# A weight ring with a fourth output tile outside it, paired modulation chunks, later raw loads and fewer waits, in a streaming trunk on one NeuronCore

## The chip, the core and the metric

The kernel runs on one NeuronCore of a Trainium2 chip. The metric is the device time of one launch in microseconds (us), and lower is better. TensorE (PE) multiplies matrices; VectorE (DVE), ScalarE (ACT) and GpSimd (POOL) do the elementwise work; SyncE (SP) issues every DMA from one queue, in the order in which the program lists them, and waits on semaphores between them.

## What is computed

One inference step of two layers over 2048 prompt tokens and 32 sample tokens, with a model width of 1024, all in float32. Layer 0 is a pooling mixer, layer 1 is sliding-window attention. Scale, shift and gate of each layer come from a modulation, a vector-matrix product with a 1024 x 3072 matrix for each layer.

```python
def trunk(x, c, sample):
    for i in range(DEPTH):                                    # DEPTH = 2
        shift, scale, gate = modulation(c, ada_w[i], ada_b[i])   # silu(c) @ ada_w + ada_b, in three
        h = rms_norm(x, norm_g[i]) * (1 + scale[:, None]) + shift[:, None]
        if i % 2 == 0:      # u, gate = h @ w_in; pooled windows of u; z = pooled @ w_grp
            y, st = pool_mixer(...)   # y = (z * scale * silu(gate)) @ w_out
        else:               # q, k, v, gate = h @ w_in; banded attention with sinks and ALiBi
            y, kw, vw = attn_...(...) # y = (o * silu(gate)) @ w_out
        x = x + gate[:, None] * y
    return rms_norm(x, final_g), pool states, k windows, v windows
```

## The kernel before

**Tiles and units.** The 2048 tokens are worked in four parts of 512; part 0 also carries the 32 sample tokens and is cut into two blocks of 272 columns. First the pooling layer runs over parts 0 to 3, then attention runs over parts 0 to 3: eight stages. A weight tile is 128 output channels by 1024 inputs. A unit is one weight tile against one block of tokens: eight k-steps, and in each of them three matmuls (`split_product`, L921), because float32 is made of a high and a low half of weights and of activations: hi x hi, hi x lo, lo x hi. A full unit is thus 24 matmuls of 512 columns.

**A pooling stage** goes through four groups g. Each group has two u units (u0, u1), two gate units (gate0, gate1), and two short z units (six matmuls each) that share one small `grp` tile; after the four groups come eight output units. **An attention stage** has four groups of kv, q0, q1, g0, g1 units, with the scores (S), transposes and products of the attention items between them, and then eight output units (`aout` 0 to 7). The first four of them (three in the `ps_u` banks, one in `ps_s`) run k-steps 0 to 5 while the last items are still being finished, then k-steps 6 and 7, and only then follows the fifth.

**The weight ring.** Four slots (`RING`) of `w_hi` and `w_lo` hold split tiles. Tile j goes to slot j % 4, and it is asked for (step `WL`) right behind the last unit that uses tile j - 4: SP waits until that unit is done (`tile_used`, L735 to L748 and L774) and then issues two DMAs of 512 KB (`fetch_tile`, L779 and L780). In the first use of a tile it is loaded raw, split by ACT and POOL and stored to DRAM (`keep_tile`); from then on both halves are fetched from there.

**The early split.** The first 24 tiles of attention (`fore`: kv, q, gate tiles and `aout` 0 to 3) are split during pooling stages 1 to 3, eight in each: step FL loads a raw tile into one of two buffers (`fore_raw`, L742, L744 and L748), FW splits it (ACT, then POOL in place), FS stores both halves (L840, L841). FL of tile i + 2 waits until FS of tile i has landed, since it overwrites its buffer. In a group, FW comes behind u0 and gate0, FS behind u1 and gate1, each FS followed at once by the FL of the tile two further on.

**The modulation** is read in 48 chunks of 512 KB (L792). 16 come ahead of the first stage; the other 32, eight in each pooling stage, go through three buffers: one ADA step is eight small matmuls with a chunk (L952), and on SP the ADA step of chunk i issues the load of chunk i + 2. Steps ADA stand behind u0, u1 and gate0 of groups 0 and 1, and behind u1 and gate0 of group 2.

**What sets the order.** Nothing is scheduled at run time: class `Schedule` writes one list of steps, and each engine walks that list and does its share. SP too takes its steps in list order, so a wait on SP holds all DMAs behind it. On PE every unit waits for its bank, its weights (`w_fetched`, or `w_hi_ready` and `w_lo_ready`) and, at each k-step, for both halves of the activations, for instance:

```python
n = KT * u["s"] + k + 1
pe.wait_ge(h_hi_ready, n)
pe.wait_ge(h_lo_ready, n)
```

Of the kernel before, what the change touches and what calls it, by code (L numbers as in the profile page):

```python
# [18 lines left out]
F32 = mybir.dt.float32  # L19
# [6 lines left out]
P = 128  # L26
# [53 lines left out]
class Schedule:  # L80
# [10 lines left out]
    def __init__(self):  # L91
# [25 lines left out]
        load_after = {self.last_unit[j - RING]: j for j in range(RING, len(self.tiles))}  # L117
        steps, self.steps = self.steps, []
        for st in steps:
            self.steps.append(st)  # L120
            if st[0] == "U" and st[3] == KT and st[1] in load_after:
                self.steps.append(("WL", load_after[st[1]]))
# [77 lines left out]
    def pool(self, p):  # L200
# [46 lines left out]
        for g in range(GROUPS):  # L247
            for i in range(2):
                emit(self.group(p, self.tile(("pin", 2 * g + i)), "u", n=2 * g + i, g=g, i=i))
                if i == 0:  # L250
                    self.early(p, 2 * g)
                else:
                    self.early_out(p, 2 * g)
                if g < 2:
                    self.ada(1)
                elif g == 2 and i:
                    self.ada(1)
                if i == 1:
                    s.append(("PL", p, g, 0))
            late, lower = [], []  # L260
            for i in range(2):
# [176 lines left out]
def trunk_kernel(nc, I, O):  # L438
# [3 lines left out]
    with ExitStack() as ctx:  # L442
# [92 lines left out]
        w_fetched = [sem(f"w_fetched{i}") for i in range(RING)]  # L535
# [31 lines left out]
        kept, home, fore = sched.kept, sched.home, sched.fore  # L567
# [12 lines left out]
        def keeps(j):  # L580

            return sum(1 for i in kept if i <= j and i % RING == j % RING and own(i))
# [7 lines left out]
        def fetches(j):  # L590

            return sum(1 for i in range(j + 1) if i % RING == j % RING and not own(i))
# [11 lines left out]

        def bank_of(u):
# [6 lines left out]
        loads, per_slot = [], [0] * RING  # L612
        for j, t in enumerate(tiles):
            if own(j):
                per_slot[j % RING] += 32 if t[0] == "kv" else 16
            loads.append(per_slot[j % RING])
# [113 lines left out]
        def _(sp):  # L730
# [20 lines left out]
            def load_tile(j):  # L751

                t = tiles[j]
                if j >= RING:
                    tile_used(sp, j - RING)
                    if own(j - RING):
                        sp.wait_ge(w_kept[j % RING], 32 * keeps(j - RING))
                load_raw(t, w_raw[:, j % RING, :], raw_loaded[j % RING])

            def keep_tile(j):  # L760
# [4 lines left out]
                sp.dma_start(w_hi_dram[i, :, 0:n], w_hi[:, j % RING, 0:n].bitcast(F32)).then_inc(w_kept[j % RING], 16)  # L765
                sp.dma_start(w_lo_dram[i, :, 0:n], w_lo[:, j % RING, 0:n].bitcast(F32)).then_inc(w_kept[j % RING], 16)

            def fetch_tile(j):

                i, n = kept.index(home[j]), width[j]  # L770
                tile_used(sp, j - RING)
# [3 lines left out]
                else:  # L775
                    sp.wait_ge(w_kept[home[j] % RING], 32 * keeps(home[j]))
                if own(j - RING):
                    sp.wait_ge(w_kept[j % RING], 32 * keeps(j - RING))
                sp.dma_start(w_hi[:, j % RING, 0:n].bitcast(F32), w_hi_dram[i, :, 0:n]).then_inc(w_fetched[j % RING], 16)  # L779
                sp.dma_start(w_lo[:, j % RING, 0:n].bitcast(F32), w_lo_dram[i, :, 0:n]).then_inc(w_fetched[j % RING], 16)  # L780
# [124 lines left out]
        def _(pe):  # L905
# [26 lines left out]
            for st in steps:  # L932
# [68 lines left out]
                elif kind == "U":  # L1001
# [22 lines left out]
                    if own(j):  # L1024
                        pe.wait_ge(w_hi_ready, splits(j))
                        pe.wait_ge(w_lo_ready, splits(j))
                    else:
                        pe.wait_ge(w_fetched[j % RING], 32 * fetches(j))
                    bank = ps_u[u["bank"]] if u["bank"] < 3 else ps_s[:, u["bank"] - 3, :]
                    slot = j % RING  # L1030
                    if u["kind"] == "z":
# [4 lines left out]
                            (w_hi[:, slot, a:a + P], w_lo[:, slot, a:a + P], q_st[:, k, c0:c0 + w], q_st[:, 2 + k, c0:c0 + w])  # L1036
                            for k, a in enumerate(at)])
                    else:
# [7 lines left out]
                        for k in range(k_from, k_to):  # L1046

                            if u["kind"] != "out":
# [7 lines left out]
                            else:  # L1056
# [4 lines left out]
                                (w_hi[:, slot, k * P:(k + 1) * P], w_lo[:, slot, k * P:(k + 1) * P],  # L1061
# [450 lines left out]
        def _(act):  # L1512
# [6 lines left out]
            for st in steps:  # L1519
                kind = st[0]  # L1520
                if kind == "W":

                    j = st[1]
                    act.wait_ge(raw_loaded[j % RING], loads[j])
                    A(w_hi[:, j % RING, 0:width[j]], w_raw[:, j % RING, 0:width[j]], ACT.Copy).then_inc(w_hi_ready, 1)  # L1525
# [242 lines left out]
        def _(pool):  # L1768
# [8 lines left out]
            for st in steps:  # L1777
                kind = st[0]
                if kind == "W":
# [4 lines left out]
                    pool.wait_ge(raw_loaded[j % RING], loads[j])  # L1784
                    G.tensor_tensor(w_lo[:, j % RING, 0:width[j]], w_raw[:, j % RING, 0:width[j]],  # L1785
                                    w_hi[:, j % RING, 0:width[j]].bitcast(F32), ALU.subtract).then_inc(w_lo_ready, 1)
# [107 lines left out]
```

## Time and profile before

| | |
|---|---|
| time, median of 3 runs | 1662.85 us (1662.7 to 1666.46) |
| the profiled execution's own time | 1663.97 us |
| its span, first to last instruction | 1662.2 us, mean granted clock 0.983 |
| PE busy | 1572.7 us (95%) |
| DVE, ACT, POOL busy | 826.7, 729.9, 421.6 us (50%, 44%, 25%) |
| DMA moved | 342.10 MB, 58.4% of 16 engines' span on SP's queue |
| mean DMA rate, pooling stages 1, 2, 3 | 293, 287, 277 GB/s (share 0.83, 0.81, 0.79) |
| mean DMA rate, attention stages 1, 2, 3 | 152, 154, 135 GB/s (share 0.43, 0.43, 0.39) |

The first stage begins at 50 us, pooling stages 1 to 3 lie between 220 and 748 us, attention after that; its stage 1 ends near 1205, stage 2 near 1415. A busy PE is not a PE at its peak: matmuls overlap in the records, and what counts is how far their starts are apart. The profile counts an engine's idle time from the modelled end of its last matmul, some 0.17 us later than the next one could have started. A wait that the profile puts down to "issue" on PE is one that it can't name a releaser for; a DMA's landing is often behind it.

### The profile page before, as it was taken

The numbers are of one execution on the slowest core, as the hardware profiler recorded it, in microseconds if no ns is written. First come the engines' busy times: TensorE is split into PE (matmuls) and PEld (weight loads), VectorE is DVE, ScalarE is ACT, GpSimd is POOL, SyncE is SP. The second block draws the span as 40 slices with busy tenths as digits, with TensorE's granted clock in tenths as the row PEclk, the third lists the DMA queues.
The fourth block names the chain that finished last, engine by engine and source line by source line (L and its number), as shares of the span: only waits on it lengthen the run. The fifth ranks groups of instructions, "written<-read, shape, count | busy, mean of one in ns | idle before, by whom it ended". The sixth has DMA issues, their size and how long they took to land.

```text
span 1662.2 us, 28381 instructions
## 1 busy us (share of the span) xinstructions
PE 1572.7 (95%) x9355; PEld 1319.7 (79%) x9355; DVE 826.7 (50%) x2154; ACT 729.9 (44%) x1618; POOL 421.6 (25%) x403
## 2 busy tenths in 40 slices
PE   5899999989999999999889899999899998999997
PEld 2899987777777877888888798888788887888876
DVE  2556335323434344336666634666346664366651
ACT  3444433223232333235555454656436664456642
POOL 0342421112111211112222241333213333123332
PEclk9899999999999999999999999999999999999998
DMA  8787788886888778962222275334463334643313
GB/s 286 267 291 262 265 302 289 299 318 229 281 325 286 272 278 289 335 242 103 103 104 102 102 256 188 142 129 153 151 203 128 128 137 167 211 149 129 131 67 135
DMA packets 174519, 342.10 MB, mean 206 GB/s; under 512 B 22127, under 2 KB 89023, under 8 KB 174126
## 3 DMA queue, kind: packets, MB, share of 16 engines
q1 hardware_dynamic: 174382, 340.29, 58.4%
q8 instruction: 84, 1.38, 0.3%
q14 instruction: 53, 0.43, 0.1%
HBM read 266.13 MB, written 74.31 MB: 205 GB/s over the span
## 4 chain that ended last, share of the span: by engine, by line
PE 75%; DMA 7%; DVE 6%; ACT 4%; issue 3%; SPq 2%; POOL 1%; POOLq 0%; DVEq 0%; ACTq 0%
PE ps_u L921 59%; DMA w_lo_kept<-fore_raw 4%; PE ps_o L1153 4%; PE ps_s L1107 3%; PE ps_t L1126 3%; ACT work L1726 1%; DMA work<-in_x_prompt_dram 1%; DVE work L1453 1%; PE ps_s L921 1%; ACT ps_u L1625 1%; PE ps_s L952 1%; DMA chunks<-in_ada_w_dram 1%; DMA w_raw<-in_pool_w_out_dram 1%; PE ps_t L1166 1%; DVE ps_u L1308 1%
## 5 line engine op out<-in xcount | busy, mean ns | idle before, releaser
L921 PE MATMUL ps_u<-h_all_hi,w_hi 128*128 128x512 f32 (+2 forms) x1440 | 520.4, 361 | 11.9 <-DVE h_all_lo L1238 4.4
L921 PE MATMUL ps_u<-h_all_lo,w_hi 128*128 128x512 f32 (+2 forms) x1440 | 511.2, 355 | 0.0
L921 PE MATMUL ps_u<-h_all_hi,w_lo 128*128 128x512 f32 (+2 forms) x1440 | 510.8, 355 | 0.0
L921 PEld LDWEIGHTS ps_u<-h_all_hi,w_hi 128*128 128x128 f32 x1440 | 274.2, 190 | 66.5 <-issue 22.7
L921 PEld LDWEIGHTS ps_u<-h_all_hi,w_lo 128*128 128x128 f32 x1440 | 274.1, 190 | 36.9
L921 PEld LDWEIGHTS ps_u<-h_all_lo,w_hi 128*128 128x128 f32 x1440 | 274.1, 190 | 34.5
L1308 DVE TENSOR_TENSOR ps_u<-ps_u,rstd_b 128x512 f32<-128x512 f32 (+1 forms) x180 | 107.1, 596 | 274.4 <-PE ps_u L921 266.9
L921 PE MATMUL ps_u<-y_hi,w_hi 128*128 128x512 f32 (+1 forms) x600 | 218.4, 364 | 16.0 <-issue 10.6
L1866 POOL TENSOR_TENSOR work<-work,recip 128x512 f32<-128x512 f32 (+2 forms) x136 | 132.9, 997 | 360.3 <-DVE recip L1470 360.3
L921 PE MATMUL ps_u<-y_hi,w_lo 128*128 128x512 f32 (+1 forms) x600 | 213.2, 355 | 0.0
L921 PE MATMUL ps_u<-y_lo,w_hi 128*128 128x512 f32 (+1 forms) x600 | 212.6, 354 | 0.0
L1726 ACT ACTIVATE work<-work,neg_max 128x256 f32<-128x256 f32 (+1 forms) x272 | 132.1, 487 | 109.1 <-DVE sink_arg L1461 109.1
L1625 ACT ACTIVATE ps_u<-ps_u,wb 128x272 f32<-128x272 f32 (+1 forms) x144 | 73.2, 521 | 160.1 <-DVE ps_u L1308 159.5
L921 PEld LDWEIGHTS ps_u<-y_hi,w_hi 128*128 128x128 f32 x600 | 114.2, 190 | 36.8 <-issue 20.3
L921 PEld LDWEIGHTS ps_u<-y_lo,w_hi 128*128 128x128 f32 x600 | 114.3, 190 | 16.4 <-issue 1.4
L921 PEld LDWEIGHTS ps_u<-y_hi,w_lo 128*128 128x128 f32 x600 | 113.7, 189 | 16.1
L1792 POOL TENSOR_TENSOR fore_raw<-fore_raw,fore_hi 128x1024 fp32r<-128x1024 f32 x24 | 57.5, 2397 | 252.0 <-ACT fore_hi L1529 252.0
L1785 POOL TENSOR_TENSOR w_lo<-w_raw,w_hi 128x1024 fp32r<-128x1024 f32 (+1 forms) x32 | 72.3, 2262 | 145.6 <-ACT w_hi L1525 145.6
L1453 DVE CUSTOM_DVE_ANT_0 work<-ps_s,bias 128x256 f32<-128x256 f32 (+1 forms) x272 | 95.7, 407 | 1.4
L1817 POOL TENSOR_TENSOR acc<-acc,sq 128x512 f32<-128x512 f32 (+1 forms) x48 | 62.7, 1307 | 130.3 <-ACT sq L1667 130.3
L1845 POOL TENSOR_TENSOR y_lo<-acc,y_hi 128x256 fp32r<-128x256 f32 (+1 forms) x72 | 49.2, 684 | 182.2 <-ACT y_hi L1752 182.2
L1625 ACT ACTIVATE work<-ps_u,wb 128x512 f32<-128x512 f32 (+3 forms) x48 | 25.4, 549 | 136.4 <-DVE ps_u L1308 136.4
(210 smaller groups left out, 2237.1 us busy)
## 6 DMA issues: line engine op xcount, KB each, us to landing
w_hi<-w_hi_kept SPq DMA_DIRECT2D x180, 512.0 KB, 4.1
w_lo<-w_lo_kept SPq DMA_DIRECT2D x180, 512.0 KB, 5.2
chunks<-in_ada_w_dram SPq DMA_DIRECT2D x32, 512.0 KB, 6.1
w_hi_kept<-w_hi SPq DMA_DIRECT2D x28, 512.0 KB, 3.3
w_lo_kept<-w_lo SPq DMA_DIRECT2D x28, 512.0 KB, 4.4
w_hi_kept<-fore_hi SPq DMA_DIRECT2D x24, 512.0 KB, 9.1
w_lo_kept<-fore_raw SPq DMA_DIRECT2D x24, 512.0 KB, 10.0
w_raw<-in_pool_w_in_dram SPq DMA_DIRECT2D x16, 512.0 KB, 5.9
```

Of the source, the lines that this page charges most:

```text
L921: last = nc.tensor.matmul(out, w, x, start=(i == 0), stop=(i == n - 1))
L1107: last = nc.tensor.matmul(score_block(it, at + e, k0), q_st[half, q, c0:c0 + P], k[half, d, kc], start=(i == 0), stop=(i == 2))
L1126: last = nc.tensor.transpose(t_flat[:, o:o + P], work[:, a % 2, at * 256 + kt * P:at * 256 + (kt + 1) * P], ident[:, :])
L1153: last = nc.tensor.matmul(ps_o[:, n * 256:n * 256 + 256], v_st[:, d, t + kt, :], pt[:, o:o + 256], start=(i == 0), stop=(i == 2 * len(kts) ...
L1308: V.tensor_tensor(bank[:, 0:w], bank[:, 0:w], rstd_b[:, c0:c0 + w], ALU.mult).then_inc(scaled, 1)
L1453: last = V.tensor_tensor_reduce(out=out, in0=src, in1=b, scale=HEAD_DIM ** -0.5, scalar=LOWEST, op0=ALU.add, op1=ALU.max, accum_out=row_ma ...
L1625: last = A(dst, src, ACT.Identity, bias=wb[:, u["n"], v:v + 1])
L1726: A(x, x, ACT.Exp, bias=neg_max[r, d, at:at + 1], accum_out=row_sum[r, d, at:at + 1])
L1785: G.tensor_tensor(w_lo[:, j % RING, 0:width[j]], w_raw[:, j % RING, 0:width[j]], w_hi[:, j % RING, 0:width[j]].bitcast(F32), ALU.subtract) ...
L1792: G.tensor_tensor(raw.bitcast(F32R), raw, fore_hi[:, i % FORE, :].bitcast(F32), ALU.subtract).then_inc(fore_lo_ready, 1)
L1817: G.tensor_tensor(acc[:, 0:w], acc[:, 0:w], sq[:, 0:w], ALU.add).then_inc(acc_ready, 1)
L1866: last = G.tensor_tensor(x, x, recip[r, d, 2 * n:2 * n + 2].unsqueeze(2).to_broadcast([r.stop - r.start, 2, w]), ALU.mult)
```

## The change

The change has four parts.

- **Raw tiles later.** FL leaves `early_out` and gets a function of its own, `early_next`. The FL that followed FS behind u1 now comes behind gate0; the one behind gate1 now comes behind the two z units.
- **Chunks in pairs.** ADA steps come two at a time, behind u1 and behind gate0 of groups 0 and 1; group 2 has none.
- **`aout` 3 outside the ring.** The fourth output tile of attention gets a slot of its own (number 4), which lies in `q_st`, the queries' buffer. It is asked for behind the last score step S of its stage, and SP waits there for that step. The ring's next tiles move up by one: `aout` 4 takes the place in the ring that `aout` 3 had, and is asked for behind the last gate unit.
- **Repeated waits left out.** A unit's weights are waited for once, at its first block and first k-step, and the activations' halves only in the first unit of each stage and its first output unit.

```diff
+            if t != ("aout", 3):
+                n, at = at, (at + 1) % RING
+            self.slot.append(n)
+            self.before.append(held.get(n))
+            held[n] = j
+        load_after = {("U", self.last_unit[self.before[j]]): j for j in range(len(self.tiles)) if self.slot[j] < RING and self.before[j] is not None}
+            if t == ("aout", 3):
+                p = self.units[self.last_unit[j]]["p"]
+                load_after[("S", max(x["a"] for x in self.items if x["p"] == p))] = j
...
         if p:
-            i = EARLY // 3 * (p - 1) + n
-            self.steps.append(("FS", i))
-            if i + FORE < EARLY:
-                self.steps.append(("FL", i + FORE))
+            self.steps.append(("FS", EARLY // 3 * (p - 1) + n))
+
+    def early_next(self, p, n):
+
+        i = EARLY // 3 * (p - 1) + n + FORE
+        if p and i < EARLY:
+            self.steps.append(("FL", i))
...
-                if g < 2:
-                    self.ada(1)
-                elif g == 2 and i:
-                    self.ada(1)
+                if g < 2 and i:
+                    self.ada(2)
...
                 if i == 0:
+                    self.early_next(p, 2 * g)
                     self.early(p, 2 * g + 1)
...
-                    if g < 3:
-                        self.ada(1)
-                    else:
+                    if g < 2:
+                        self.ada(2)
+                    elif g == 3:
...
             s.extend(late + lower + [("E2", late[0][1])])
+            self.early_next(p, 2 * g + 1)
...
+        q_flat = q_st[:, :, :].rearrange("p a c -> p (a c)")
+        tile_hi = [w_hi[:, i, :] for i in range(RING)] + [q_flat[:, 0:KT * P]]
+        tile_lo = [w_lo[:, i, :] for i in range(RING)] + [q_flat[:, KT * P:2 * KT * P]]
...
+                if slot == RING:
+                    p = units[sched.last_unit[j]]["p"]
+                    sp.wait_ge(s_ready, sum(1 for x in items if x["p"] <= p))
...
-                    if own(j):
+                    if u["b"] == 0 and k_from == 0 and own(j):
...
-                            if u["kind"] != "out":
+                            if u["u"] not in stage_first:
+                                pass
+                            elif u["kind"] != "out":
```

On SP, in pooling stage 2, the DMAs from the end of group 0's u0 on stand like this before (`w_hi<-w_hi_kept` and `w_lo<-w_lo_kept` are a tile's fetch, `w_hi_kept<-fore_hi` and `w_lo_kept<-fore_raw` an FS, `fore_raw<-` an FL, `chunks<-` the load of a chunk):

```order
L779 DMA w_hi<-w_hi_kept 128x512
L780 DMA w_lo<-w_lo_kept 128x512
L792 DMA chunks<-in_ada_w_dram 128x2x512
L779 DMA w_hi<-w_hi_kept 128x1024
L780 DMA w_lo<-w_lo_kept 128x1024
L840 DMA w_hi_kept<-fore_hi 128x1024
L841 DMA w_lo_kept<-fore_raw 128x1024
L748 DMA fore_raw<-in_attn_w_in_dram 128x8x64 x2
L792 DMA chunks<-in_ada_w_dram 128x2x512
L779 DMA w_hi<-w_hi_kept 128x1024
L780 DMA w_lo<-w_lo_kept 128x1024
L792 DMA chunks<-in_ada_w_dram 128x2x512
```

And now, on the same engine at the same place:

```order
L806 DMA w_hi<-w_hi_kept 128x512
L807 DMA w_lo<-w_lo_kept 128x512
L806 DMA w_hi<-w_hi_kept 128x1024
L807 DMA w_lo<-w_lo_kept 128x1024
L867 DMA w_hi_kept<-fore_hi 128x1024
L868 DMA w_lo_kept<-fore_raw 128x1024
L819 DMA chunks<-in_ada_w_dram 128x2x512 x2
L806 DMA w_hi<-w_hi_kept 128x1024
L807 DMA w_lo<-w_lo_kept 128x1024
L771 DMA fore_raw<-in_attn_w_in_dram 128x8x64 x2
L819 DMA chunks<-in_ada_w_dram 128x2x512 x2
```

The FL moved from behind the FS to behind the next fetch; of the three chunk loads, each two ADA steps ahead of its use, two now stand behind the FS and two behind the FL.

On PE, in pooling stage 1, group 0, the end of u1 and the begin of gate0 stood so before, with the waits in brackets:

```order
L921 MATMUL ps_u<-h_all_lo,w_hi 128x512
L921 MATMUL ps_u<-h_all_hi,w_lo 128x512
L952 MATMUL ps_s<-chunks,c_wide 32x256 [waits ada_loaded4]
L952 MATMUL ps_s<-chunks,c_wide 32x256 x3
L921 MATMUL ps_u<-h_all_hi,w_hi 128x512 [waits h_hi_ready,h_lo_ready,w_fetched2,x_new]
L921 MATMUL ps_u<-h_all_lo,w_hi 128x512
L921 MATMUL ps_u<-h_all_hi,w_lo 128x512
L921 MATMUL ps_u<-h_all_hi,w_hi 128x512 [waits h_lo_ready,h_hi_ready]
```

Now, from the same place on:

```order
L979 MATMUL ps_s<-chunks,c_wide 32x256 [waits ada_loaded6,x_put_dve,x_put_act]
L979 MATMUL ps_s<-chunks,c_wide 32x256 x3
L979 MATMUL ps_s<-chunks,c_wide 32x256 [waits ada_loaded4]
L979 MATMUL ps_s<-chunks,c_wide 32x256 x3
L948 MATMUL ps_u<-h_all_hi,w_hi 128x512 [waits w_fetched2,x_new]
L948 MATMUL ps_u<-h_all_lo,w_hi 128x512
L948 MATMUL ps_u<-h_all_hi,w_lo 128x512
L948 MATMUL ps_u<-h_all_hi,w_hi 128x512
```

Two chunks stand behind the unit instead of one, the next two follow after one unit (gate0), and the second k-step carries no wait.

On SP, at the end of attention stage 1, behind its last gate unit, before:

```order
L779 DMA w_hi<-w_hi_kept 128x1024
L780 DMA w_lo<-w_lo_kept 128x1024
L855 DMA x_even<-x_mid 128x4x512 x2
L779 DMA w_hi<-w_hi_kept 128x1024
L780 DMA w_lo<-w_lo_kept 128x1024
```

Now:

```order
L806 DMA w_hi<-w_hi_kept 128x1024
L807 DMA w_lo<-w_lo_kept 128x1024
L882 DMA x_even<-x_mid 128x4x512 x2
L806 DMA q_st<-w_hi_kept 128x1024
L807 DMA q_st<-w_lo_kept 128x1024
L806 DMA w_hi<-w_hi_kept 128x1024
L807 DMA w_lo<-w_lo_kept 128x1024
```

The first fetch was that of `aout` 3 and is now that of `aout` 4; `aout` 3 comes after the next part's x, into `q_st`, and the last fetch of each list is the one that waits for `aout` 0's unit.

## Rows read from the trace of the kernel before

**Rows 1.** Waits of PE, whole run: us in total, times, longest us

```profile
PE ps_u L921 <- issue: 15.0, 8, 3.8
```

**Rows 2.** The same view for 220 to 750 us, pooling stages 1 to 3

```profile
PE ps_u L921 <- issue: 5.4, 5, 2.1
PE ps_s L952 <- DMA chunks<-in_ada_w_dram: 4.4, 3, 1.9
PE ps_s L977 <- DMA work<-in_x_prompt_dram: 2.8, 2, 2.1
PE ps_u L921 <- ACT ps_u L1625: 2.5, 2, 1.5
```

**Rows 3.** Waits of SP's queue, the same stretch and columns

```profile
SPq L744 <- DMA w_lo_kept<-fore_raw: 144.2, 15, 10.7
```

**Rows 4.** PE in order of time, attention stage 1: start, us, [idle before]

```profile
1155.70 0.28 PE L1107 MATMUL ps_s<-k_lo,q_st 64*128 64x256 f32 x2
...
1170.41 0.48 PE L921 MATMUL ps_s<-y_hi,w_hi 128*128 128x512 f32 x1
...
1182.81 0.40 PE L921 MATMUL ps_s<-y_hi,w_lo 128*128 128x512 f32 x1
1187.02 0.77 PE L921 MATMUL ps_u<-y_hi,w_hi 128*128 128x512 f32 x1 [3.81 <-issue]
1187.58 0.63 PE L921 MATMUL ps_u<-y_lo,w_hi 128*128 128x512 f32 x1
1188.01 0.63 PE L921 MATMUL ps_u<-y_hi,w_lo 128*128 128x512 f32 x1
```

**Rows 5.** SP there (start, us), and landings (KB, us from issue to landing)

```profile
1181.14 0.33 SPq L779 DMA_DIRECT2D w_hi<-w_hi_kept  x1
1181.52 1.60 SPq L780 DMA_DIRECT2D w_lo<-w_lo_kept  x1
...
w_hi<-w_hi_kept SPq DMA_DIRECT2D x1, 512.0 KB, 4.4
w_lo<-w_lo_kept SPq DMA_DIRECT2D x1, 512.0 KB, 5.4
```

**Rows 6.** Stretches: length, busy PE (count), PEld, DVE, ACT, POOL, clock, DMA, GB/s

```profile
336.00:339.40 3.40, 2.91 (x7) 2.36 (x8) 2.83 (x6) 1.58 (x2) 0.39 (x1) 0.50 1.02 358
506.70:513.50 6.80, 5.15 (x12) 4.11 (x13) 5.16 (x7) 1.58 (x2) 2.36 (x1) 0.50 1.00 378
1185.90:1192.70 6.80, 5.68 (x13) 4.46 (x14) 1.42 (x2) 3.48 (x6) 2.55 (x2) 0.50 1.03 419
```

**Rows 7.** PE in order of time, within a unit of pooling stage 2

```profile
431.12 0.39 PE L921 MATMUL ps_u<-h_all_hi,w_lo 128*128 128x512 f32 x1
431.35 0.39 PE L921 MATMUL ps_u<-h_all_hi,w_hi 128*128 128x512 f32 x1
```

**Rows 8.** Chain of waits, pooling stage 2, group 0: start, us, what

```profile
414.36 0.57 PE ps_s L952 x8
414.93 5.76 PE ps_u L921 x24
```

**Rows 9.** PE ahead of the first stage, two chunks in a row

```profile
19.81 0.64 PE L952 MATMUL ps_u<-x_odd,c_wide 128*32 128x256 f32 x8
20.27 0.61 PE L952 MATMUL ps_u<-work,c_wide 128*32 128x256 f32 x8
```

**Rows 10.** SP in order of time, pooling stages 2 and 3, behind group 0's u1

```profile
414.39 0.32 SPq L779 DMA_DIRECT2D w_hi<-w_hi_kept  x1
...
423.33 1.01 SPq L748 DMA_DIRECT2D fore_raw<-in_attn_w_in_dram  x2
...
583.04 0.32 SPq L779 DMA_DIRECT2D w_hi<-w_hi_kept  x1
...
593.44 0.38 SPq L744 DMA_DIRECT2D fore_raw<-in_attn_w_in_dram  x1
```

**Rows 11.** A chunk's landing in stage 0, issued at 97.14 us: KB, us

```profile
chunks<-in_ada_w_dram SPq DMA_DIRECT2D x1, 512.0 KB, 7.3
```

More of the change, by code:

```diff
@@ L116, in __init__ @@
         self.steps = [s for s in self.steps if s[0] != "W" or (s[1] < len(self.tiles) and self.home[s[1]] == s[1] and s[1] not in self.fore)]
-        load_after = {self.last_unit[j - RING]: j for j in range(RING, len(self.tiles))}
+        self.slot, self.before, held, at = [], [], {}, 0
+        for j, t in enumerate(self.tiles):
+            n = RING
+            if t != ("aout", 3):
[4 more added lines that the diff above has]
+        load_after = {("U", self.last_unit[self.before[j]]): j for j in range(len(self.tiles)) if self.slot[j] < RING and self.before[j] is not None}
+        for j, t in enumerate(self.tiles):
+            if t == ("aout", 3):
+                p = self.units[self.last_unit[j]]["p"]
+                load_after[("S", max(x["a"] for x in self.items if x["p"] == p))] = j
         steps, self.steps = self.steps, []
@@ L120, in __init__ @@
             self.steps.append(st)
-            if st[0] == "U" and st[3] == KT and st[1] in load_after:
-                self.steps.append(("WL", load_after[st[1]]))
+            if (st[0] == "S" or st[0] == "U" and st[3] == KT) and st[:2] in load_after:
+                self.steps.append(("WL", load_after[st[:2]]))
         seen = {}
@@ L534, in trunk_kernel @@
         w_kept = [sem(f"w_kept{i}") for i in range(RING)]
-        w_fetched = [sem(f"w_fetched{i}") for i in range(RING)]
+        w_fetched = [sem(f"w_fetched{i}") for i in range(RING + 1)]
         w_hi_ready, w_lo_ready, ada_done = sem("w_hi_ready"), sem("w_lo_ready"), sem("ada_done")
@@ L580, in keeps @@
         def keeps(j):
-            return sum(1 for i in kept if i <= j and i % RING == j % RING and own(i))
+            return sum(1 for i in kept if i <= j and slot_of[i] == slot_of[j] and own(i))
         def fore_done(eng):
@@ L590, in fetches @@
         def fetches(j):
-            return sum(1 for i in range(j + 1) if i % RING == j % RING and not own(i))
+            return sum(1 for i in range(j + 1) if slot_of[i] == slot_of[j] and not own(i))
         def tile_used(eng, j):
@@ L603, in ada_slot @@
             return (i % LANDING, i // LANDING + 1) if i < first else (LANDING + (i - first) % CHUNKS, (i - first) // CHUNKS + 1)
+        stage_first = set()
+        for stage in range(2 * PARTS):
+            stage_first.add(next(u["u"] for u in units if u["s"] == stage))
+            stage_first.add(next(u["u"] for u in units if u["s"] == stage and u["kind"] == "out"))
         def bank_of(u):
@@ L610, in shifts @@
             return SHIFT if u["p"] == 0 and u["b"] == 0 and u["kind"] in ("u", "gate", "kv", "q", "agate") else 0
[L612 removed]
+        loads, per_slot = [], [0] * (RING + 1)
         for j, t in enumerate(tiles):
             if own(j):
[L615 to L616 removed]
+                per_slot[slot_of[j]] += 32 if t[0] == "kv" else 16
+            loads.append(per_slot[slot_of[j]])
         width = [2 * 2 * P if t[0] == "grp" else KT * P for t in tiles]
@@ L753, in load_tile @@
                 t = tiles[j]
[L754 to L758, printed above, removed]
+                if before_in[j] is not None:
+                    tile_used(sp, before_in[j])
+                    if own(before_in[j]):
+                        sp.wait_ge(w_kept[slot_of[j]], 32 * keeps(before_in[j]))
+                load_raw(t, w_raw[:, slot_of[j], :], raw_loaded[slot_of[j]])
             def keep_tile(j):
@@ L775, in fetch_tile @@
                 else:
[L776 to L780, printed above, removed]
+                    sp.wait_ge(w_kept[slot_of[home[j]]], 32 * keeps(home[j]))
+                sp.dma_start(tile_hi[slot][:, 0:n].bitcast(F32), w_hi_dram[i, :, 0:n]).then_inc(w_fetched[slot], 16)
+                sp.dma_start(tile_lo[slot][:, 0:n].bitcast(F32), w_lo_dram[i, :, 0:n]).then_inc(w_fetched[slot], 16)
             def load_ada(i):
@@ L1523, in _ @@
                     j = st[1]
-                    act.wait_ge(raw_loaded[j % RING], loads[j])
-                    A(w_hi[:, j % RING, 0:width[j]], w_raw[:, j % RING, 0:width[j]], ACT.Copy).then_inc(w_hi_ready, 1)
+                    act.wait_ge(raw_loaded[slot_of[j]], loads[j])
+                    A(w_hi[:, slot_of[j], 0:width[j]], w_raw[:, slot_of[j], 0:width[j]], ACT.Copy).then_inc(w_hi_ready, 1)
                 elif kind == "FW":
```

29 lines of the change are left out of this document (16 added, 13 removed).

## The prediction, made before the result was known

> **What bounds the kernel now.** I read the waits of PE first, then PE and SP in order of time around each wait, and last the stretches with a low granted clock. PE is busy for 95% of the span, so the end is set by PE's own work, its waits, and the clock at which it works. The useful number is the pitch, the distance between starts: 0.23 us for a 512-column matmul (431.12 to 431.35) [rows 7], though each is recorded as 0.39 long.
>
> Two groups of waits touch the change. In attention, PE waits for `aout` 4. Over the whole run "issue" ends 8 waits of 15.0 us; 5 of them, 5.4 us, lie in the pooling stages, so the 3 in attention are 9.6 us [rows 1, 2]. One is shown in rows 4: the last matmul of `aout` 3 starts at 1182.81 and the next unit at 1187.02. Its weights' second half was issued at 1181.52 and landed 5.4 us later, at 1186.92 [rows 5]: the releaser is the fetch. In the pooling stages four groups of waits add up to 5.4 + 4.4 + 2.8 + 2.5 = 15.1 us in 5 + 3 + 2 + 2 = 12 waits [rows 2]. The row that names ACT belongs to them too: around it ACT has finished and a fetch has not. These fetches and loads are late because SP stands still: one FL line alone waits 144.2 us, 15 times, for an FS to land [rows 3], and every DMA behind it in the list waits with it.
>
> The third thing is the clock. After some of these waits the granted clock is 0.50, the 1.2 GHz level, while PE works on [rows 6]. There the pitch is 0.43 (1187.58 to 1188.01) [rows 4], so each matmul loses 0.43 − 0.23 = 0.20 us.
>
> **Attention: `aout` 3 outside the ring, a gain.** `aout` 4 is now asked for behind the last gate unit, more than 10 us ahead of its use, and the wait goes. Between starts it is 1187.02 − 1182.81 − 0.23 = 3.98 us, against 3.81 in the row: the row counts from a modelled end, and 0.17 comes on top per wait. So 9.6 + 3 × 0.17 = **10.1**. What is late next? `aout` 3 itself: it may be fetched when the last S is over, about 1155.98, is used at 1170.41 [rows 4], and a pair of DMAs needs 1.60 + 5.4 us at most [rows 5]. That leaves about 7 us, so it costs nothing unless SP comes late to that step. `aout` 5 is still asked for behind `aout` 0, as `aout` 4 was: 1181.1, landed 1186.9, needed at 1187.0 + 5.8 less the 4.0 gained, so about 1188.8; 1.9 us are left. With the wait goes the fall of the clock: 13 matmuls behind the wait of stage 1 [rows 6] and 9 behind that of the last stage, a fall of the same kind, (13 + 9) × 0.20 = **4.4**.
>
> **Raw tiles later, a gain.** An FL now comes behind gate0 or behind the two z units. Six or more microseconds pass between FS and FL in the first place, so the FS has nearly landed. Behind z some wait stays on SP, but the next fetch isn't asked for until u0 of the next group ends, 12 × 0.23 + 5.76 = 8.5 us after FS; SP holds it by under 2 us. FW of the raw tile comes at least 5.76 + 2.76 + 5.76 = 14.3 us later, so ACT and POOL have it in time. I take all 12 waits as gone: 15.1 + 12 × 0.17 = **17.1**. The least is 9.8, the first two groups of rows 2, if the other two have a reason of their own. The clock falls behind three of these waits: 7 and 12 matmuls [rows 6], and a third one like the first, (7 + 12 + 7) × 0.20 = **5.2**.
>
> **Chunks in pairs, a gain and the large loss.** A single ADA step holds PE for 0.57 us [rows 8], and the unit behind it takes 5.76 − 24 × 0.23 = 0.24 more than its pitch. In a pair the second step costs 20.27 − 19.81 = 0.46 [rows 9]. A pair saves 2 × (0.57 + 0.24) − (0.57 + 0.46 + 0.24) = 0.35 us; 16 pairs are **5.6**.
>
> The loss: the three chunk buffers allow a load only when a chunk before it has been used. The second pair of a group stands one unit behind the first. Its two loads are asked for behind u1, and on SP they stand behind a fetch (two DMAs) and an FS (two DMAs). PE is there after a pair and a gate unit: 0.57 + 0.46 + 5.76 = 6.8 us. When do the loads land? In before, FL waits there for just those four DMAs: from 414.39 to 423.33, 8.94 us, and in stage 3 from 583.04 to 593.44, 10.40 us [rows 10]. A further 512 KB comes 1.38 us later (landings 1181.14 + 4.4 and 1181.52 + 5.4) [rows 5]. So the first chunk is there after 10.3 us, a wait of 3.5, and the second 1.38 later, a wait of 1.38 − 0.57 = 0.8: **4.3** per place. In stage 3 it is 11.8 − 6.8 = 5.0 and 0.8, **5.8**. There are two such places (groups 0 and 1) in each of stages 1 to 3: 2 × (4.3 + 4.3 + 5.8) = **28.8**. No row shows this wait itself. From below, a chunk landed 7.3 us after its issue in stage 0 [rows 11]; issued behind four other DMAs, 0.38 us each (1181.14 to 1181.52) [rows 5], that gives 7.3 + 1.5 − 6.8 = 2.0, and 2.8 with the second. From above it is stage 3's 5.8 everywhere. I take the middle since rows 10 show the very place. In stage 0 no FS stands ahead, and the 2 places there cost about 0.5 each: **1** (0 to 3).
>
> The clock may fall behind these waits. Of the three waits in attention, some 3 us each, two were followed by it, of the 12 shorter ones in pooling three. The price was 1.4 to 2.6 where it fell; over six places I take 1.6 each, **9.6** (0 to 15.6).
>
> **Repeated waits left out.** Some 244 units lose seven k-steps' waits. A matmul that carries them starts 0.23 us behind the last [rows 7], as those without do, so the wait is hidden by the matmul ahead of it. From above it's what a step might lose unseen, half of the 0.01 us that the rows resolve, by 1,700 steps, 8 us; I take **2** (0 to 8), near the lower end where the rows are.
>
> **The sum.** Gains: 10.1 + 4.4 + 17.1 + 5.2 + 5.6 + 2 = 44.4. Losses: 28.8 + 1 + 9.6 = 39.4. Net −5.0, from the profiled execution's 1663.97 to 1659.0. That execution lies 1.1 above the median, so I forecast 1658.
>
> **Rivals.** (1) **Slower: the paired loads come late everywhere by stage 3's measure.** Each place then costs 5.8 and a long fall of the clock, 13 matmuls, 2.6. Six places are 50.4, and 1 for stage 0: 51.4 − 44.4 = +7.0, so 1670. It decides from (44.4 − 1) / 6 = 7.2 us per place, where the gains are used up; the forecast has 6.4. For it: two more loads are in the queue than before, and the DMA share is over 0.99 in three stretches [rows 6]. Against it: two of three stages showed 8.94.
>
> (2) **Chunks overtake the stores.** In rows 5 two DMAs asked one after the other land in that order, and the sum goes by that order. If a load does not wait for the two stores ahead of it, it lands 2 × 1.38 = 2.8 us earlier: 0.7 + 0.8 = 1.5 us in stages 1 and 2 and 3.0 in stage 3, 12.0 in all, and with waits so short the clock stays. Then −44.4 + 12.0 + 1 = −31.4, and 1631. Against it: 144.2 us of waits behind stores say nothing of loads that follow, and no row shows a load passing a store. The Trainium skill, page *DMA: Bandwidth & Descriptors*, section *Queues, rings and completion order*, says that completion is "not FIFO per issuing engine", though descriptors are consumed in ring order; by the first half this rival would hold, by the second hardly. The order in rows 5 agrees with the second.
>
> (3) **`aout` 3 isn't fetched ahead of the wait.** If SP comes late to its step, `aout` 4's wait is only exchanged for one of `aout` 3, and 10.1 + 4.4 stay: 1658 + 14.5 = 1672. Against it are the 7 us of slack.
>
> (4) **The repeated waits lie on the path**: up to 8 instead of 2, 1652.
>
> **How the numbers follow.** A measurement here tells 0.3%, 5 us, from no change. Chances: the forecast's case, places of 3.0 to 7.2 us, 0.60; rival 1, 0.20; rival 2, 0.12; rival 3, 0.03; rival 4, 0.05. The forecast's case spans 1662.9 − 43.4 + 6 × 3.0 = 1638 to 1663, or 1667 where the other gains fall short by 4; half of it, 0.30, is faster by over 0.3%, 0.27 is within, and 0.03 slower. With rivals 2 and 4 and a little, faster is 0.47; rival 1 gives 0.17 to slower and 0.03 to no change, so slower is 0.23 and the same 0.30. The range of 8 in 10 goes from 1638 to 1670: it leaves out the most of rival 2 below and rival 3 and the worst of rival 1 above.
>
> **What would show it.** PE waits for `chunks` at six places of the ADA line, 3.5 to 5 us each with the second; under 2 would be rival 2, over 7 with the clock rival 1. Behind them a granted clock of 0.50 in some. SP's waits for `w_lo_kept<-fore_raw` at FL fall to less than half. No "issue" wait of 3 us between `aout` 3 and `aout` 4, nor one ahead of `aout` 3. The pitch within a unit stays 0.23; 0.225 would be rival 4. The forecast is wrong if fetches in pooling still come late, or if waits of the score stretches move.

## The result, and the profile after

The changed kernel is slower, by about half a per cent. Its median over 7 runs is 1675.09 us (1671.11 to 1679.5), that of before over 7 runs 1664.44; the ratio is 1.0055 (95% interval 1.0036 to 1.0074). Measured again with the experiments it is 1673.93 us over 10 runs against 1665.72 us over 19, ratio 1.0042 (1.0021 to 1.0063). The profiled execution took 1676.21 us, of which the span is 1674.4, at a mean granted clock of 0.974. Forecast were 1658 us and a range from 1638 to 1670.

The waits of PE in the whole run (us in total, times, longest), its first lines and the one of the output units:

```profile
PE ps_s L979 <- DMA chunks<-in_ada_w_dram: 30.6, 16, 5.4
PE ps_o L1182 <- issue: 9.0, 12, 1.9
...
PE ps_u L948 <- POOL y_lo L1874: 5.3, 4, 1.6
```

The 15.0 us of "issue" ahead of units [rows 1] have left the list, the pooling stages' waits of [rows 2] too, and a group of 16 waits for chunks now leads it. Where they lie is told by the same view for 50 to 220 us (stage 0) and for 220 to 750 us (stages 1 to 3), one line of each:

```profile
PE ps_s L979 <- DMA chunks<-in_ada_w_dram: 3.3, 4, 1.1
```

```profile
PE ps_s L979 <- DMA chunks<-in_ada_w_dram: 27.3, 12, 5.4
```

Twelve waits in stages 1 to 3 are six pairs. One of them, group 0 of stage 1, shows PE in order of time (start, us, operation, idle before):

```profile
259.51 0.40 PE L948 MATMUL ps_u<-h_all_hi,w_lo 128*128 128x512 f32 x1
263.31 1.08 PE L979 MATMUL ps_s<-chunks,c_wide 128*32 128x256 f32 x8 [3.40 <-DMA chunks<-in_ada_w_dram]
265.35 1.08 PE L979 MATMUL ps_s<-chunks,c_wide 128*32 128x256 f32 x8 [0.96 <-DMA chunks<-in_ada_w_dram]
266.36 0.80 PE L948 MATMUL ps_u<-h_all_hi,w_hi 128*128 128x512 f32 x1
```

The eight small matmuls of a chunk take 1.08 us here and not 0.57 as in [rows 8]: the granted clock is 0.50 from 262.6 to 269.4, its 1.2 GHz level. SP asked for these two chunks as the forecast had it, behind a fetch and an FS, with FL now behind the next fetch (SP in order of time):

```profile
253.19 0.32 SPq L806 DMA_DIRECT2D w_hi<-w_hi_kept  x1
253.55 0.43 SPq L807 DMA_DIRECT2D w_lo<-w_lo_kept  x1
254.08 0.38 SPq L867 DMA_DIRECT2D w_hi_kept<-fore_hi  x1
254.50 0.43 SPq L868 DMA_DIRECT2D w_lo_kept<-fore_raw  x1
254.97 1.70 SPq L819 DMA_DIRECT2D chunks<-in_ada_w_dram  x2
259.94 0.34 SPq L806 DMA_DIRECT2D w_hi<-w_hi_kept  x1
260.32 0.43 SPq L807 DMA_DIRECT2D w_lo<-w_lo_kept  x1
262.04 0.38 SPq L767 DMA_DIRECT2D fore_raw<-in_attn_w_in_dram  x1
```

and they landed so (KB, median us from issue to landing):

```profile
chunks<-in_ada_w_dram SPq DMA_DIRECT2D x2, 512.0 KB, 9.1
w_hi<-w_hi_kept SPq DMA_DIRECT2D x1, 512.0 KB, 4.3
w_lo<-w_lo_kept SPq DMA_DIRECT2D x1, 512.0 KB, 5.9
w_hi_kept<-fore_hi SPq DMA_DIRECT2D x1, 512.0 KB, 6.8
w_lo_kept<-fore_raw SPq DMA_DIRECT2D x1, 512.0 KB, 7.5
```

The four DMAs ahead land at 257.5, 259.5, 260.9 and 262.0, in the order of asking, and only then the two chunks, 8.3 and 9.9 us after their issue (9.1 is the middle of the two). PE starts with the first at 263.31, 10.1 us after the fetch was issued, where the forecast had 10.3.

The waits of SP's queue in 220 to 750 us, the lines that stand against [rows 3]:

```profile
SPq L767 <- DMA w_lo_kept<-fore_raw: 52.3, 15, 5.3
SPq L765 <- DMA w_lo_kept<-fore_raw: 13.2, 4, 5.2
SPq L771 <- DMA w_lo_kept<-fore_raw: 11.3, 3, 5.0
```

The line that waited for 144.2 us now waits for 52.3; the three together still wait 22 times, 76.8 us in all. And in attention the place of [rows 4], the end of `aout` 3 and the begin of `aout` 4 in stage 1:

```profile
1208.03 0.39 PE L948 MATMUL ps_s<-y_hi,q_st 128*128 128x512 f32 x1
1208.26 0.39 PE L948 MATMUL ps_s<-y_lo,q_st 128*128 128x512 f32 x1
1208.49 0.39 PE L948 MATMUL ps_s<-y_hi,q_st 128*128 128x512 f32 x1
1208.72 0.40 PE L948 MATMUL ps_u<-y_hi,w_hi 128*128 128x512 f32 x1
```

The last matmul with a weight from `q_st` and the next unit's first one are 0.23 us apart, as any two within a unit. Of the wait of 3.98 us nothing is left.

In pooling stages 1 to 3 of this execution six stretches of 6.8 us have a low granted clock, one at each pair of waits. Two of them (columns as in [rows 6]):

```profile
436.60:443.40 6.80, 6.16 (x26) 3.62 (x27) 1.04 (x2) 1.36 (x2) 2.35 (x1) 0.50 0.98 311
...
644.80:651.60 6.80, 6.39 (x26) 3.86 (x27) 1.63 (x3) 2.17 (x3) 2.36 (x1) 0.50 0.71 254
```

### The profile page after: what moved, and what is told of

Its sections match the earlier page's. It is cut to its first block, busy times and chain, and to the rows that moved or that the text cites. A ratio compares the mean times of both kernels' runs of the same rounds, so it can differ in the third digit from the quotient of the medians.

```text
span 1674.4 us, 26333 instructions
## 1 busy us (share of the span) xinstructions
PE 1578.7 (94%) x9355; PEld 1327.0 (79%) x9355; DVE 826.7 (49%) x2154; ACT 729.7 (44%) x1618; POOL 421.9 (25%) x403
## 4 chain that ended last, share of the span: by engine, by line
PE 74%; DMA 7%; DVE 6%; ACT 6%; issue 4%; SPq 2%; POOL 1%; DVEq 0%; ACTq 0%; POOLq 0%
PE ps_u L948 58%; DMA chunks<-in_ada_w_dram 4%; PE ps_o L1182 4%; PE ps_s L1136 3%; PE ps_t L1155 3%; ACT work L1755 1%; PE ps_s L948 1%; DVE work L1482 1%; ACT ps_u L1654 1%; DVE ps_u L1337 1%; DMA w_raw<-in_pool_w_out_dram 1%; POOL w_lo L1814 1%; PE ps_t L1195 1%; ACT silu_g L1670 1%; DVE ps_o L1512 1%
## 5 line engine op out<-in xcount | busy, mean ns | idle before, releaser
L948 PE MATMUL ps_u<-y_hi,w_hi 128*128 128x512 f32 (+1 forms) x584 | 212.6, 364 | 5.6 <-POOL y_lo L1874 5.3
L948 PE MATMUL ps_u<-y_hi,w_lo 128*128 128x512 f32 (+1 forms) x584 | 208.0, 356 | 0.0
L948 PE MATMUL ps_u<-y_lo,w_hi 128*128 128x512 f32 (+1 forms) x584 | 207.7, 356 | 0.0
L948 PEld LDWEIGHTS ps_u<-y_hi,w_lo 128*128 128x128 f32 x584 | 111.1, 190 | 15.6
L1874 POOL TENSOR_TENSOR y_lo<-acc,y_hi 128x256 fp32r<-128x256 f32 (+1 forms) x72 | 49.2, 683 | 182.2 <-ACT y_hi L1781 182.2
```

Of the source, the lines that this page charges most:

```text
L948: last = nc.tensor.matmul(out, w, x, start=(i == 0), stop=(i == n - 1))
```

## The experiments

Lengths of stages tell most here. A stage is counted from the start of its first unit's first matmul to that of the next stage, and the last one to the start of PE's last matmul. By this count pooling stages 1 to 3 of before go from 227.9 to 728.9 us and attention stage 1 ends at 1212.9, so the stretch from 220 to 750 us contains those three stages and a little more. The table sums up what the runs below showed; "start" is the time at which stage 0 begins, one profiled execution each, and the last column the median of all runs.

| kernel | start | stage 0 | pooling 1 to 3 | attention 0 | attention 1 to 3 | median us |
|---|---|---|---|---|---|---|
| before | 49.9 | 178.0 | 501.0 | 261.1 | 665.3 | 1665.7 |
| changed | 52.6 | 187.0 | 516.7 | 261.0 | 650.2 | 1675.1 |
| changed, later on (`after_again`) | 51.7 | 188.1 | 516.5 | 262.7 | 649.8 | 1673.9 |
| `x_no_pairs` | 50.1 | 178.7 | 478.8 | 261.0 | 650.2 | 1632.0 |
| `x_spread` | 52.2 | 182.2 | 474.8 | 261.9 | 650.1 | 1629.5 |
| `b_pairs` | 52.3 | 183.3 | 547.1 | 261.0 | 664.3 | 1716.2 |
| `b_aout` | 51.8 | 179.3 | 501.2 | 261.9 | 649.7 | 1652.4 |
| `b_later` | 51.9 | 177.2 | 477.3 | 262.7 | 663.5 | 1643.0 |
| `x_loads_first` | 52.7 | 185.6 | 497.3 | 261.9 | 649.8 | 1657.1 |
| `x_keep_waits` | 52.8 | 183.3 | 512.9 | 261.9 | 651.5 | 1671.1 |
| `x_single0` | 52.7 | 178.6 | 515.0 | 261.0 | 650.1 | 1669.4 |
| `x_best` | 50.4 | 178.5 | 474.7 | 261.0 | 649.9 | 1624.6 |
| `x_best_waits` | 51.0 | 183.4 | 473.2 | 261.0 | 650.3 | 1624.2 |
| `x_best_again` | 52.1 | 178.5 | 473.2 | 261.9 | 650.3 | 1625.1 |

The theory was that the pairs alone carry the loss and the three other parts give what was forecast. The rival was that a part of the missing 15 us lies in those parts.

**`x_no_pairs`: chunks one at a time again.**

```diff
-                if g < 2 and i:
-                    self.ada(2)
+                if g < 2:
+                    self.ada(1)
+                elif g == 2 and i:
+                    self.ada(1)
...
-                    if g < 2:
-                        self.ada(2)
-                    elif g == 3:
+                    if g < 3:
+                        self.ada(1)
+                    else:
```

> The changed kernel with the chunks one at a time at the places of before; the three other parts stay. Theory P (the pairs are the whole loss: six waits of PE for chunks of about 5.4 us each and two of about 2.3 us in stage 0, plus a lower clock behind them): all of these waits go, the gains of the other parts stay (15 us in attention, about 19 us of waits and 5 of clock in the pooling stages), so the time falls to 1622 to 1634 us. Theory O (some of the 15 us by which the forecast failed come from the other parts, the later raw loads or the missing waits of units): 1640 us or more, and the first pooling stage stays some 5 us longer than before.

Measured: 1631.95 us, ratio to before 0.9801 (0.9774 to 0.9829). The rival falls in the form put on record, 1640 us or more. A smaller part of it stays: the three other parts give 1665.72 − 1631.95 = 33.8 us, where 38.8 were forecast. Of PE's waits in 220 to 750 us none for a DMA is left; these are the first lines of that view, and both lie in attention, which begins at 707.6 us here:

```profile
PE ps_s L1138 <- DVE sink_arg L1492: 1.3, 1, 1.3
PE ps_t L1157 <- POOL work L1897: 1.2, 1, 1.2
```

Pooling stages 1 to 3 are 37.9 us shorter than in the changed kernel, stage 0 8.4.

**`b_pairs`: before, with the pairs alone** (the lines just shown, the other way round).

> The kernel before with the chunks in pairs and nothing else. There an FL stands directly behind the FS ahead of the paired loads, so SP holds them until the stores have landed. Theory P: each of the six places costs more than in the changed kernel, some 7 to 9 us with the second chunk, and the time rises by 35 to 60 us, to 1700 to 1725 us. Theory O: the pairs cost only what was forecast, 28.8 + 9.6 + 1 - 5.6 = 34 us less the 4.4 us of chunk waits of before, 1694 us or less.

Measured: 1716.18 us, ratio 1.0304 (1.0281 to 1.0327). With FL still directly behind FS, the place shown above from 259.51 on looks so (PE in order of time, then SP):

```profile
265.29 1.08 PE L950 MATMUL ps_s<-chunks,c_wide 128*32 128x256 f32 x8 [7.79 <-DMA chunks<-in_ada_w_dram]
266.59 1.08 PE L950 MATMUL ps_s<-chunks,c_wide 128*32 128x256 f32 x8 [0.21 <-DMA chunks<-in_ada_w_dram]
```

```profile
252.10 0.43 SPq L839 DMA_DIRECT2D w_lo_kept<-fore_raw  x1
259.67 0.38 SPq L742 DMA_DIRECT2D fore_raw<-in_attn_w_in_dram  x1
260.09 1.09 SPq L790 DMA_DIRECT2D chunks<-in_ada_w_dram  x2
```

SP stands from 252.5 to 259.7, and the chunks are asked for only then: 8.0 us at one place, inside the 7 to 9 of the theory. Over stages 1 to 3 PE waits twice as long for chunks as in the changed kernel:

```profile
PE ps_s L950 <- DMA chunks<-in_ada_w_dram: 53.5, 12, 9.5
```

**`b_aout` and `b_later`: before, with one of these parts alone.** In `b_aout` the slot of the fourth tile differs and what follows from it (when it is fetched, and the ring's next tiles), in `b_later` the place of FL. Of each edit only the lines that decide are shown:

```diff
+            if t != ("aout", 3):
+                n, at = at, (at + 1) % RING
...
```

```diff
...
+                    self.early_next(p, 2 * g)
...
+            self.early_next(p, 2 * g + 1)
```

> The kernel before with the fourth output tile in the queries' buffer and nothing else. Theory P: the three waits of 3 to 4 us ahead of the fifth output unit go with the low clock behind two of them, 1648 to 1651 us (the forecast's 10.1 + 4.4). Theory O: less than 10 us of gain, because the fetch of the fourth tile or the next part's x comes later.

> The kernel before with the raw tiles asked for a unit later and nothing else. The forecast gave this part 17.1 us of waits and 5.2 us of clock, so 1642 to 1648 us beside a median of some 1667 us for before on this day's runs; from the stages of the two kernels without pairs, 22 us. If the later loads collide with the single chunks, PE keeps waits for chunks and the gain is under 15 us.

Measured: 1652.44 us, ratio 0.9924 (0.9894 to 0.9954), and 1642.98 us, ratio 0.9864 (0.9843 to 0.9886). In the stages, `b_aout` takes 665.3 − 649.7 = 15.6 us out of attention 1 to 3 and nothing elsewhere, `b_later` 501.0 − 477.3 = 23.7 out of pooling 1 to 3. Forecast were 14.5 and 22.3. (1652.44 lies just above the 1648 to 1651 us expected of `b_aout`.)

**`x_loads_first`: the two loads ahead of the two stores on SP.** PE's order is the same.

```diff
-                else:
-                    self.early_out(p, 2 * g)
                 if g < 2 and i:
                     self.ada(2)
+                if i:
+                    self.early_out(p, 2 * g)
```

> The changed kernel with the two ADA steps behind u1 listed ahead of the FS instead of behind it: PE's order is the same, SP asks for the two chunks ahead of the two stores. Theory Q (the wait of PE is the place of the loads in the queue: they land in order, 1.4 us for each DMA ahead): the loads land two DMAs earlier, some 2.8 us, so each of the six places falls from some 5.4 us to 2 to 3, the lower clock behind them gets rarer, and the time is 1650 to 1661 us. Theory B (the loads are late since the DMA engines are full in those stages, whatever the order): the six waits change by less than 1 us each, 1670 us or more. If loads may overtake stores, the order of asking doesn't matter either: 1670 us or more.

Measured: 1657.12 us, ratio 0.9955 (0.9936 to 0.9974), beside 1673.93 for the changed kernel. PE's waits for chunks in 220 to 750 us fall from 27.3 to 16.0, that is 2.7 a place, and three of the six low stretches of the clock are gone, while the other three are 3.4 us long instead of 6.8. The waits and the landings at the place shown above:

```profile
PE ps_s L979 <- DMA chunks<-in_ada_w_dram: 16.0, 12, 2.8
```

```profile
chunks<-in_ada_w_dram SPq DMA_DIRECT2D x2, 512.0 KB, 7.2
w_hi<-w_hi_kept SPq DMA_DIRECT2D x1, 512.0 KB, 3.6
w_lo<-w_lo_kept SPq DMA_DIRECT2D x1, 512.0 KB, 4.4
w_hi_kept<-fore_hi SPq DMA_DIRECT2D x1, 512.0 KB, 8.4
w_lo_kept<-fore_raw SPq DMA_DIRECT2D x1, 512.0 KB, 9.3
```

They are the same six DMAs, with the chunks at 7.2 us instead of 9.1 and the stores later instead. So the place in the queue costs 27.3 − 16.0 = 11.3 us of waits, and at these places a load doesn't overtake the stores by itself. Engines that are merely full would have left the waits as they were. The 2.7 us a place that are left stay with the loads behind the fetch alone: one unit between pair and pair is too short even so.

**`x_keep_waits`, `after_again`, and the pair `x_best_waits`, `x_best_again`: the waits left out.** In the first, all waits of units are put back:

```diff
-                    if u["b"] == 0 and k_from == 0 and own(j):
+                    if own(j):
...
-                            if u["u"] not in stage_first:
-                                pass
-                            elif u["kind"] != "out":
+                            if u["kind"] != "out":
```

> The changed kernel with all the waits of units put back. The forecast gave the missing waits 2 us (0 to 8). If they lie hidden behind the matmul ahead of them, the time is that of the changed kernel, 1675 us, within 3; if each of the 1,700 costs PE's queue something, 1678 to 1683 us.

Measured: 1671.14 us, which neither expectation covered: 4 us faster with the waits than the changed kernel had been. That could have been a price of leaving them out, or scatter, so the changed kernel was run again:

> The changed kernel once more, on one chip with the next three, since the kernel with all waits put back gave 1671 against 1675 us on another chip. Theory S (the waits for chunks and the first 50 us scatter from execution to execution by some us): 1670 to 1676 us. Theory W (leaving the waits out costs some 4 us): 1674 us or more while the kernel with them stays at 1671.

1673.93 us over 10 runs, from 1665.69 to 1677.61: this settles nothing. A kernel without chunk waits does:

> Singles in stage 0 and one pair behind u0 of each group from stage 1 on, with all the waits of units put back. No wait for chunks is left here that could scatter. Theory S: the missing waits are worth nothing, the time is that of the same kernel without them, 1624.6 us, within 2, and its stages 2 and 3 of pooling agree within 0.1 us. Theory W: some 4 us faster, 1621 us. The forecast's rival 4: up to 8 us slower, 1632 us.

> The same kernel without those waits, on the same chip: 1623 to 1627 us, as measured once, beside the one with them.

Measured: 1624.23 us with the waits, 1625.05 without; pooling stage 2 takes 158.73 and 158.74 us, stage 3 155.39 in both. `b_later` has the waits and `x_no_pairs` has not, and there the two stages take 160.10 and 160.10, 156.75 and 156.74. The missing waits are worth nothing, neither way. Stage 0 is another matter: 183.4 us in `x_best_waits` and 178.5 in `x_best_again`, with singles in both. In the longer one PE waits 3.4 us for an x tile at 210.86, and the granted clock is 0.50 for 6.8 us there; in the shorter one it waits 1.4 us and the clock stays. So stage 0 can differ by 5 us without any pair in it.

**`x_single0`: singles in stage 0 alone.**

```diff
-                if g < 2 and i:
+                if p and g < 2 and i:
                     self.ada(2)
+                elif not p and (g < 2 or g == 2 and i):
+                    self.ada(1)
...
-                    if g < 2:
-                        self.ada(2)
+                    if g < 2 + (not p):
+                        self.ada(2 if p else 1)
```

> The changed kernel with the chunks one at a time in stage 0 alone, in pairs as they are from stage 1 on. The forecast gave the pairs of stage 0 a cost of 1 us less 1.4 saved; the profiles show stage 0 4.7 to 8.4 us longer with them. Theory: 5 to 9 us below the changed kernel, 1665 to 1670 us. If the longer stage 0 is scatter of the start, it equals the changed kernel within 3 us.

Measured: 1669.42 us over 10 runs, 4.5 below `after_again` on the same chip, a little less than the 5 to 9 expected; the scatter of ten runs each leaves some 2 to 7. Stage 0 takes 178.6 instead of 188.1. So the pairs cost stage 0 4.5 us by the medians and 9.5 by one pair of profiles, but those 9.5 aren't all theirs: they hold the wait for the x tile (2.3 us against 1.4) and a fall of the clock behind it, which `x_best_waits` shows without pairs. Over all profiles, the six with pairs in stage 0 take 182.2 to 188.1 us for it, seven of the eight without take 177.2 to 179.3, and `x_best_waits` 183.4.

**`x_spread` and `x_best`: pairs where their loads have time.** `x_spread` has one pair behind u0 of each group; `x_best` does so from stage 1 on and has singles in stage 0:

```diff
-                if g < 2 and i:
+                if p and i == 0:
                     self.ada(2)
+                elif not p and (g < 2 or g == 2 and i):
+                    self.ada(1)
...
-                    if g < 2:
-                        self.ada(2)
+                    if not p and g < 3:
+                        self.ada(1)
                     elif g == 3:
```

> The changed kernel with one pair of chunks behind u0 of each of the four groups instead of two pairs in groups 0 and 1: every load is asked for a whole group (some 25 us) ahead of its use. Theory P: no wait for chunks is left, and the pairs' saving of 0.35 us each stays, so 3 to 6 us below the kernel without pairs, 1617 to 1630 us. Theory O: 1640 us or more. If a pair in itself costs something (a stall behind sixteen small matmuls), it lies above the kernel without pairs.

> The changed kernel with the chunks one at a time in stage 0, as before, and from stage 1 on one pair behind u0 of each group. In the kernel with pairs behind u0 everywhere stages 1 to 3 were 1.3 us shorter each than without pairs, but stage 0 was 3.5 us longer. Theory: stage 0 as without pairs and the others as with them, so 3 to 5 us below the kernel without pairs, 1624 to 1629 us. If the longer stage 0 was only the scatter of the start, it equals the kernel with pairs everywhere, 1629 us.

Measured: 1629.45 us, ratio 0.9778 (0.9759 to 0.9796), and 1624.64 us, ratio 0.9758 (0.9732 to 0.9784), which beats before by 41 us and the changed kernel by some 49. No wait for chunks is left in either. In `x_spread` stage 0 is 3.5 us longer than in `x_no_pairs`; PE waits there for `silu_g` 2.9 us in 7 waits, against 0.7 in 4, which is 2.2 of them. In stages 2 and 3 `x_best` is 1.37 and 1.35 us shorter than `x_no_pairs`: four pairs by 0.34.

## Why the prediction was wrong

The sign was wrong. The mechanism of the large loss was the one named, waits for the second pair's chunks behind the stores; the term for stage 0 was mis-sized by far, and smaller misses went the same way. Point by point:

- **`aout` 3 outside the ring**, 10.1 + 4.4 = 14.5: right. 15.6 us of stages in `b_aout`. The fetch into `q_st` was issued at 1182.09 at the latest, took 7.0 us and was used at 1196.10, so the 7 us of slack were there and rival 3 fell.
- **Raw tiles later**, 17.1 + 5.2 = 22.3: right. 23.7 in `b_later`, and the waits that were put down to ACT went with the rest. One step on the way was off: FS had not "nearly landed" when FL came, as the 22 waits of 76.8 us on SP show. PE has no wait for a DMA left in stages 1 to 3 of `b_later` all the same.
- **What a pair saves**, 0.35 us: right, 0.34 in `x_best`.
- **Repeated waits left out**, 2 us (0 to 8): nothing. The value at the end where the rows stood was the true one; rival 4 fell.
- **The six second pairs of stages 1 to 3**: 28.8 of waits and 9.6 of clock, less 4.2 saved by 12 pairs, 34.2; measured 516.7 − 478.8 = 37.9. Between starts the places hold PE for 4.2 to 6.1 us, 30.6 in all, near the 28.8. The remainder, 37.9 + 4.2 − 30.6 = 11.5, is put down to the clock: 1.9 us a place instead of 1.6. It fell at every place, for 6.8 us, and took the second chunk's small matmuls (1.08 instead of 0.57) with it, which the price by full-width matmuls had left out. This part is not the same in every execution. Four profiles have these pairs: the changed kernel, `after_again`, `x_single0` and `x_keep_waits`, with 516.7, 516.5, 515.0 and 512.9 us, and in them the low stretch is 6.8 us at six, five, four and two of the six places and 3.4 at the others. The last one gives 34.1, the forecast.
- **Stage 0, the step that failed.** It stood at 1 us (0 to 3), less 1.4 saved, with the reason that no FS stands ahead, and without any price for the clock. But a store of two halves and a raw tile stand there, three DMAs. SP in order of time behind u1 of group 0, whose last matmuls start at 68.2:

```profile
67.97 0.32 SPq L788 DMA_DIRECT2D w_hi_kept<-w_hi  x1
68.34 0.42 SPq L789 DMA_DIRECT2D w_lo_kept<-w_lo  x1
68.86 0.68 SPq L758 DMA_DIRECT2D w_raw<-in_pool_w_in_dram  x1
69.59 2.00 SPq L819 DMA_DIRECT2D chunks<-in_ada_w_dram  x2
```

and PE at the pair behind gate0:

```profile
75.45 0.29 PE L948 MATMUL ps_u<-h_all_hi,w_lo 128*128 128x272 f32 x1
76.84 0.64 PE L979 MATMUL ps_s<-chunks,c_wide 128*32 128x256 f32 x8 [1.10 <-DMA chunks<-in_ada_w_dram]
78.12 1.03 PE L979 MATMUL ps_s<-chunks,c_wide 128*32 128x256 f32 x8 [0.64 <-DMA chunks<-in_ada_w_dram]
79.08 0.60 PE L948 MATMUL ps_u<-h_all_hi,w_hi 128*128 128x274 f32 x1
```

The chunk is there at 76.8, 7.2 us from its issue, very nearly the 7.3 of [rows 11]; the issue comes 1.2 us behind the unit's end at 68.4, and PE is there at 75.6, 7.2 us behind that end. By these times the 7.3 of the row in hand gives a wait of 1.3 us, and the second chunk's comes on top of it; the row was used as a bound for other places instead, and for its own place the price was guessed. The four waits of stage 0, 3.3 us in the view, are 4.3 between starts, where 1 was forecast. Behind the pair shown the clock falls for 3.4 us here too, and the waits for `silu_g` are 1.5 us instead of the 0.8 of before. Together the pairs cost stage 0 a net 4.5 us by the medians (up to 9.5 between two profiles), where 1 − 1.4 = −0.4 was forecast.

- **The sum.** By the medians of all runs (1665.72 for before, 1673.93 for `after_again`) the miss is 8.2 + 5.0 = 13.2 us, and it has three parts. The pairs of stage 0 cost 4.5 instead of −0.4: 4.9. Those of stages 1 to 3 cost 1669.42 − 1631.95 = 37.5 instead of 34.2: 3.3. The three other parts give 33.8 instead of 38.8: 5.0, of which 2 are the waits that are worth nothing. Why the rest of these 5.0 is missing isn't settled, since `b_aout` and `b_later` alone give 14.9 and 23.1 beside the runs of before that were taken with them; the four runs of `x_no_pairs` lie between 1627 and 1636 us, and the first 50 us alone took 49.9 to 52.8 in the profiles, with before at the lowest.
- **The rivals.** Rival 1 had the sign, but its condition didn't hold. It had 8.4 us per place in stages 1 to 3; measured were (37.9 + 4.2) / 6 = 7.0 in the changed kernel and 6.4 in `x_keep_waits`, below the 7.2 from which it was to decide. The pairs of stage 0 and the gains that fell short made the kernel slower, so that its sign was in part luck. Rival 2, chunks that overtake stores, fell: at all six places of the changed kernel both chunks land behind both stores, and in `x_loads_first`, where they are asked for first, ahead of both. The order in [rows 5] could not tell this, because both halves of a fetch count up one semaphore (`w_fetched`), so that the profile's two landings come in that order whatever happened; the chunks have semaphores of their own. The Trainium skill, page *DMA: Bandwidth & Descriptors*, section *Queues, rings and completion order*, has descriptors consumed in ring order on each engine, and completion not FIFO per issuing engine. The landings at the six places agree with the first half; a completion out of order shows at none of them.
- **The range** ended at 1670: the loss of stage 0 was bounded at 3 us, where 4.5 + 1.4 = 5.9 were measured, and the other gains were allowed to fall short by 4 us, where they fell short by 5.

## What to carry to other kernels

A load whose buffer comes free one step before its use is only as early as the distance to that use. When steps are put together in pairs, look at the second pair, whose loads have lost a unit of time, and count every DMA that stands ahead of them in the queue. Gains from waits that go could be read from the trace to within a microsecond or two here (14.5 and 15.6, 22.3 and 23.7); a new wait must be priced at every place where it can arise, the first stage with its other DMAs included, and with the clock that falls behind it. Some 1,700 waits on semaphores that were long satisfied cost nothing here, where a 0.23 us matmul covers each of them.

## What the runs showed of the hardware

- At the six places of the changed kernel, stores to DRAM and loads from it, 512 KB each and asked by one engine, landed in the order of asking. At the place shown, two chunks behind two stores landed 8.3 and 9.9 us after their issue, and with the order turned round (`x_loads_first`) 6.8 and 7.6, while the second store went from 7.5 to 9.3.
- The granted clock went to 0.50 for 6.8 us at each of the six places where PE waited 4.2 to 6.1 us for chunks, and for 3.4 us at three of the six when it waited 2.7 us a place (`x_loads_first`). In `x_keep_waits`, with 24.8 us of these waits instead of 27.3, it was 3.4 us at four of the six, so the same place can have either.
- Attention stage 2 took 213.64 to 213.67 us in all eleven profiles with `aout` 3 outside the ring, so that differences of a few hundredths could be read there, though whole runs of one kernel scatter by some 10 us.
